# RWKV mixer in an encoder kernel: key order alternating by head pair, with whole-chunk handoffs

## What is computed

```
def step(S, inp):
    r_t, w_t, k_t, v_t, kk_t, b_t = inp
    sa = jnp.einsum('bhvk,bhk->bhv', S, -kk_t)
    S = S * w_t[:, :, None, :] + sa[..., None] * b_t[:, :, None, :] + v_t[..., None] * k_t[:, :, None, :]
    return S, jnp.einsum('bhvk,bhk->bhv', S, r_t)
...
y = head_norm(y, ln_g, ln_b, RW_GN_EPS)
y = y + jnp.sum(r * k * r_k.astype(F32), axis=-1, keepdims=True) * v
y = y.reshape(B, T, RW_WIDTH) * jax.nn.silu(g.astype(F32))
return y.astype(h.dtype) @ w_out
```

## Time and profile before

| | us |
|---|---|
| median of 3 runs | 1469.68 (1467.86 to 1470.78) |
| profiled execution | 1469.67 |
| its span | 1467.5 |
| TensorE busy | 1360.3 (93%) |
| VectorE busy | 717.9 (49%) |
| ScalarE busy | 400.5 (27%) |
| GpSimd busy | 90.6 (6%) |
| mean granted clock of TensorE | 0.975 |

### The profile page before, as it was taken

One profiled execution on the slowest core, in us unless ns is written; L12 is line 12 of the kernel. 1 busy time (PEld: TensorE's weight loads), 2 busy tenths in 40 slices (PEclk: granted clock), 3 DMA queues, 4 the chain that ended last, 5 costly groups with the idle time before them and its releaser, 6 DMA issues. The chain is left out here.

```text
span 1467.5 us, 23757 instructions
## 1 busy us (share of the span) xinstructions
PE 1360.3 (93%) x10291; PEld 715.9 (49%) x10291; DVE 717.9 (49%) x1388; ACT 400.5 (27%) x900; POOL 90.6 (6%) x82
## 2 busy tenths in 40 slices
PE   5999999999798999879899989998999999998887
PEld 3444444488444444564434436544444444477633
DVE  5784656855642002261345023434684765954552
ACT  1114243165301011460122053501113244055401
POOL 0000240100000000000000000000000152000000
PEclk9999999999899999999999989998999999999999
DMA  6222222001400222101222221123322222101211
GB/s 208 72 72 57 60 71 61 27 4 61 176 0 1 72 86 72 58 2 58 73 60 84 72 57 29 50 65 87 107 62 68 65 61 63 43 4 61 83 52 57
DMA packets 111183, 92.45 MB, mean 63 GB/s; under 512 B 5020, under 2 KB 99524, under 8 KB 110568
## 3 DMA queue, kind: packets, MB, share of 16 engines
q1 hardware_dynamic: 110376, 88.81, 19.9%
q10 hardware_dynamic: 704, 2.13, 0.4%
HBM read 84.64 MB, written 6.29 MB: 62 GB/s over the span
## 5 line engine op out<-in xcount | busy, mean ns | idle before, releaser
L871 PE MATMUL bank<-arena 128*128 128x512 f32 x960 | 420.1, 594 | 1.5 <-ACT arena L544 1.5
L871 PEld LDWEIGHTS bank<-arena 128*128 128x128 f32 x960 | 180.6, 190 | 224.9 <-issue 219.1
L826 PE MATMUL bank<-arena 64*64 64x64 f32 (+3 forms) x6720 | 187.3, 227 | 22.9 <-issue 16.2
L826 PEld LDWEIGHTS bank<-arena 64*64 64x64 f32 (+2 forms) x6720 | 164.2, 134 | 59.3 <-issue 48.3
L1200 PE MATMUL bank<-arena 128*128 128x512 f32 x256 | 116.3, 615 | 4.6 <-DVE arena L1165 4.6
L159 ACT ACTIVATE arena<-arena 128x1024 f32<-128x1024 f32 x20 | 21.1, 1055 | 243.1 <-DVE arena L1171 131.9
L1200 PEld LDWEIGHTS bank<-arena 128*128 128x128 f32 x256 | 50.0, 198 | 70.7 <-issue 64.3
L1664 PE MATMUL bank<-arena 128*128 128x512 f32 x160 | 71.2, 606 | 1.6 <-PEq L301 1.6
L637 DVE SCALAR_TENSOR_TENSOR arena<-arena 128x512 f32<-128x512 f32 x96 | 72.2, 803 | 0.0
L1296 PE MATMUL bank<-arena 128*128 128x512 f32 x128 | 56.8, 606 | 1.6 <-PEq L1109 1.6
L498 POOL MEMSET arena<- 128x8 f32 x2 | 0.2, 112 | 936.4 <-DVE arena L788 936.4
(11 more groups left out here) (232 smaller groups left out, 1615.3 us busy)
## 6 DMA issues: line engine op xcount, KB each, us to landing
arena<-in_rw_w_in SPq DMA_DIRECT2D x66, 512.0 KB, 4.0
arena<-in_ml_w_in SPq DMA_DIRECT2D x24, 512.0 KB, 3.8
arena<-in_sw_w_in SPq DMA_DIRECT2D x20, 512.0 KB, 3.7
arena<-in_rw_w_out SPq DMA_DIRECT2D x16, 512.0 KB, 7.4
spill<-arena SPq DMA_DIRECT2D x2, 2048.0 KB, 8.9
arena<-spill SPq DMA_DIRECT2D x2, 2048.0 KB, 8.6
arena<-in_sw_w_out SPq DMA_DIRECT2D x8, 512.0 KB, 3.7
arena<-in_ml_w_out SPq DMA_DIRECT2D x8, 512.0 KB, 3.7
```

What stands on the lines that cost most here:

```text
L826: mm = lambda out, a, b, start=True, stop=True: nc.tensor.matmul(out, a, b, start=start, stop=stop, skip_group_check=True)
L871: last = nc.tensor.matmul(bank[:, :], slot[:, k, :], mix_at[what][:, k, :], start=k == 0, stop=k == KT - 1)
```

## The change

The order of b and k in the 128 columns of a pair's keys alternates: even pairs hold b | k, odd pairs k | b. So one matmul with both keys as weights (64 rows, 128 columns) puts each result where the masks want it: two matmuls a pair instead of four, in `products_a` and `products_r`. `turn_values` makes both heads of a pair in one matmul. The right side's two parts and `solve` go by pairs of alternating parity, so that four pairs of row and column halves follow each other; they are handed over once a chunk, and the outputs from the state become a step of their own behind `solve`. `x(c + 1)` comes behind `turn_values(c + 1)`. The inverses are stored so that a chunk's block is contiguous. ACT: `keep_bkt` 2 copies instead of 6, `values` 2 instead of 4, `gather` 8 of half the size and 2 more instead of 4. POOL and DVE work on K and b in two halves by parity, and POOL's r_k product comes last. The reload of h moves to `rw_gate_out`, behind the loads of W; the add waits for it. The core of the diff, without context; the functions K(j), BB(j) and `of_parity` stand for the former slices elsewhere too:

```diff
-    KB = m.view(B_K, KT, NC, 2 * C)
-    K, BB = KB[:, :, :, C:P], KB[:, :, :, 0:C]
+    KB = m.view(B_K, KT // 2, NC * 2, P)
+    slots = m.view(B_K, KT // 2 * NC, 4, C)
+    both = lambda p, c: KB[:, p // 2, 2 * c + p % 2, :]
+    slot = lambda n: slots[:, :, n, :].rearrange("p (k c) d -> p k c d", c=NC)
+    tile_of = lambda at, j: slot(at(j % 2))[:, j // 2, :, :]
+    K_AT, B_AT = (lambda odd: 1 + odd), (lambda odd: 3 * odd)
+    K, BB = (lambda j: tile_of(K_AT, j)), (lambda j: tile_of(B_AT, j))
+    of_parity = lambda at, odd, c: slot(at(odd))[:, :, c, :]
+    parity = lambda buf, odd: buf.rearrange("p (k o) c -> p k o c", o=2)[:, :, odd, :]
+    in_parity = lambda buf, odd, c: parity(buf[:, :, span(c)], odd)
...
-            sp.wait_ge(rhs_done.handle, rhs_done.at(2 * BC))
+            sp.wait_ge(sa_done.handle, sa_done.at(NC))
+            m.load_weights(sp, n0 + 33 + SLOTS)
...
-            sp.dma_start(m.view(A_H, 4096), spill[0]).then_inc(reloaded.handle, 16)
...
-            sp.wait_ge(sa_done.handle, sa_done.at(2 * NC))
-            m.load_weights(sp, n0 + 33 + SLOTS)
-            sp.wait_ge(reloaded.handle, reloaded.at(16))
...
-                nc.gpsimd.tensor_tensor(R[:, :, span(c)], R[:, :, span(c)], K[:, :, c, :], ALU.mult).then_inc(rk_ready.handle, 1)
+                for odd in range(2):
+                    last = nc.gpsimd.tensor_tensor(in_parity(R, odd, c), in_parity(R, odd, c), of_parity(K_AT, odd, c), ALU.mult)
+                last.then_inc(rk_ready.handle, 1)
+                for odd in range(2):
+                    last = nc.gpsimd.tensor_tensor(of_parity(B_AT, odd, c), of_parity(B_AT, odd, c), parity(epi[c], odd), ALU.mult)
+                last.then_inc(b_scaled.handle, 1)
...
-                nc.gpsimd.tensor_tensor(BB[:, :, c, :], BB[:, :, c, :], epi[c], ALU.mult).then_inc(b_scaled.handle, 1)
...
-                    turned = blocks(t_bank(c, q))
-                    nc.scalar.activation(KB[:, pairs[q], c, 0:C], turned[:, :, 0:C], ACT.Copy)
-                    nc.scalar.activation(KB[HI, pairs[q], c, C:P], turned[LO, :, C:P], ACT.Copy)
-                    nc.scalar.activation(KB[LO, pairs[q], c, C:P], turned[HI, :, C:P], ACT.Copy).then_inc(bkt_evac.handle, 1)
+                    nc.scalar.activation(KB[:, 2 * q:2 * q + 2, 2 * c:2 * c + 2, :].rearrange("p a b c -> p a (b c)"),
+                                         t_bank(c, q)[:, :].rearrange("p (a b) -> p a b", a=2), ACT.Copy).then_inc(bkt_evac.handle, 1)
...
-                for g in range(4):
-                    rows, half = slice(Q * g, Q * g + Q), g % 2
-                    last = nc.scalar.activation(ad[rows, c // BC, :, KT * (c % BC):KT * (c % BC) + KT],
-                                                heads(ga[c], g // 2)[rows, :, Q * half:Q * half + Q]
-                                                .rearrange("p k c -> p c k"), ACT.Copy)
-                if c == NC - 1:
-                    last.then_inc(gathered.handle, 1)
+                at = KT * (c % BC)
+                for w in range(2):
+                    for half in range(2):
+                        for odd in range(2):
+                            mine, rows = slice(C * w + Q * half, C * w + Q * half + Q), slice(C * odd + Q * half, C * odd + Q * half + Q)
+                            nc.scalar.activation(ad[mine, c // BC, :, at + odd:at + KT:2],
+                                                 heads(ga[c], w ^ odd)[rows, odd:KT:2, Q * half:Q * half + Q]
+                                                 .rearrange("p k c -> p c k"), ACT.Copy).then_inc(gathered.handle, 1)
+                act.wait_ge(gathered.handle, gathered.at(8 * (c + 1)))
+                for odd in range(2):
+                    nc.scalar.activation(heads(ga[c], 1)[EARLIER[1 - odd], 1 - odd:KT:2, 0:Q],
+                                         heads(ga[c], 1)[EARLIER[odd], odd:KT:2, Q:C], ACT.Copy).then_inc(crossed.handle, 1)
...
-                for q in range(2):
-                    act.wait_ge(v_done.handle, v_done.at(2 * c + q + 1))
-                    nc.scalar.activation(heads(z[c], 0)[HI, pairs[q], :], quarter(m.bank[q])[HI], ACT.Copy)
-                    nc.scalar.activation(heads(z[c], 1)[LO, pairs[q], :], quarter(m.bank[q])[LO], ACT.Copy)\
-                        .then_inc(v_evac.handle, 1)
+                act.wait_ge(v_done.handle, v_done.at(c + 1))
+                for odd in range(2):
+                    rows = SIDE[1 - odd]
+                    last = nc.scalar.activation(both_heads(c, odd)[rows], wider(m.bank[0])[rows], ACT.Copy)
+                last.then_inc(v_evac.handle, 1)
...
-                for g in range(2):
-                    act.wait_ge(rhs_done.handle, rhs_done.at(2 * c + g + 1))
-                    nc.scalar.activation(rhs[:, pairs[g], :], quarter(m.bank[4 + g]), ACT.Copy, scale=-1.0)\
+                act.wait_ge(rhs_done.handle, rhs_done.at(c + 1))
+                for odd in range(2):
+                    nc.scalar.activation(parity(rhs, odd), quarter(m.bank[4 + odd]), ACT.Copy, scale=-1.0)\
...
-                for g in range(2):
-                    act.wait_ge(sa_done.handle, sa_done.at(2 * c + g + 1))
-                    for par, rows in SIDES:
-                        last = nc.scalar.activation(heads(z[c], par)[rows, pairs[g], :], quarter(m.bank[6 + g])[rows], ACT.Copy)
+                act.wait_ge(sa_done.handle, sa_done.at(c + 1))
+                for w in range(2):
+                    for odd in range(2):
+                        rows = SIDE[odd]
+                        last = nc.scalar.activation(head_of(c, odd, w ^ odd)[rows], quarter(m.bank[6 + w])[rows], ACT.Copy)
...
-                    nc.vector.transpose(tt[:, b], t32[:, b].rearrange("p t s -> p s t"))
-                    last = nc.vector.transpose(uu[:, b], t32[:, b])
+                    nc.vector.transpose(tt[:, b].rearrange("p n s -> p s n"), t32[:, b].rearrange("p t s -> p s t"))
+                    last = nc.vector.transpose(uu[:, b].rearrange("p n t -> p t n"), t32[:, b])
...
-                    rows, to, at = slice(Q * g, Q * g + Q), slice(Q * (g ^ 2), Q * (g ^ 2) + Q), Q * (g % 2)
-                    last = nc.vector.tensor_copy(u[c][to, :, at:at + Q], uu[rows, c // BC, :, KT * (c % BC):KT * (c % BC) + KT]
-                                                 .rearrange("p c n -> p n c"))
+                    rows, at = slice(Q * g, Q * g + Q), Q * (g % 2)
+                    last = nc.vector.tensor_copy(u[c][rows, :, at:at + Q], of_chunk(uu, c)[rows])
...
-                last = [None, None]
-                for slot, keys in ((0, BB), (1, K)):
-                    for par, rows in SIDES:
-                        out = (LO, HI)[par ^ slot]
-                        last[par] = mm(banks[par][out, C * p:C * p + C], keys[rows, p, c, :], query[rows, p, span(c)])
-                if p == KT - 1:
-                    for par in range(2):
-                        last[par].then_inc(inc.handle, 1)
+                for par, rows in SIDES:
+                    last = mm(banks[par][:, C * p:C * p + C], both(p, c)[rows], query[rows, p, span(c)])
+                    if p == KT - 1:
+                        last.then_inc(inc.handle, 1)
...
-                        last = nc.tensor.transpose(t_bank(c, q)[:, P * k:P * k + P], KB[:, 4 * q + k, c, :], ident)
+                        last = nc.tensor.transpose(t_bank(c, q)[:, P * k:P * k + P], both(4 * q + k, c), ident)
...
-                for q in range(2):
-                    for k in range(4):
-                        for par, rows in enumerate((HI, LO)):
-                            last = mm(m.bank[q][rows, C * k:C * k + C], V[:, 4 * q + k, span(c)], centre[:, C * par:C * par + C])
-                    last.then_inc(v_done.handle, 1)
+                for p in range(KT):
+                    last = mm(m.bank[0][SIDE[1 - p % 2], P * (p // 2):P * (p // 2) + P], V[:, p, span(c)], centre)
+                last.then_inc(v_done.handle, 1)
...
-            def x_begin(c):
+            def x(c):
...
-                    pe.wait_ge(ga_evac.handle, ga_evac.at(2 * NC))
+                    pe.wait_ge(crossed.handle, crossed.at(2 * NC))
...
+                for p in range(KT):
+                    for w in range(2):
+                        block = ga[c][EARLIER[w], 2 * p, Q:C] if w == p % 2 else ga[c][EARLIER[w], 2 * (p ^ 1) + 1, 0:Q]
+                        last = mm(x_bank[LATER[w], Q * p:Q * p + Q], block, of_chunk(tt, c)[EARLIER[w], p, :])
+                last.then_inc(x_done.handle, 1)
...
-            def x(c, p):
-                for par in range(2):
-                    last = mm(x_bank[LATER[par], Q * p:Q * p + Q], ga[c][EARLIER[par], 2 * p + par, Q:C],
-                              of_chunk(tt, c, p)[EARLIER[par]])
-                if p == KT - 1:
-                    last.then_inc(x_done.handle, 1)
...
-            def xu(c, p):
-                for par in range(2):
```

(69 more changed lines are left out.)

66 lines of the change are left out of this document (36 added, 30 removed).

## The result

The changed kernel takes 1462.31 us (median of 17 runs, 1460.65 to 1464.60), against 1469.68 for the kernel before (17 runs beside them). The ratio is 0.9948, 95% interval 0.9938 to 0.9957: faster by 0.5%, less than a third of the 24.7 us forecast and outside the range of 1436 to 1458.

A forecast was written before the change was run, and what follows sets the result against it. TensorE bounds the kernel, its chunk loop on the edge of its instruction fetch. Loop gain 25.2 us less 0.6 for the v stage makes 24.6, from 1469.68 to 1445 us; own range 1441 to 1449, whole range 1436 to 1458.

The forecast's parts named there:

- The products: Merged 64x128 instructions in `products_a` and `products_r`: 29 ns each, 0.93 us against 0.95 in the chunk loop, so nothing.
- part 1: The chunk loop of layers 1 and 4: periods fall to 9.9 us, gaining 11.8 and 13.4 us, 25.2 in all.
- part 2: The v projections alternating with `products_a`: -1.2 for POOL's earlier b, +1.5 for gather, +0.3 us a layer, range -1.5 to +3.
- Rival D: Merged products neither overlap nor hide their loads, 60 ns each: 1.92 against 0.95 us, 1474 us in all; chance 0.04.
- the ring: V stage cycle of mask, gather, exponentials, scale: its turn grows from 6.43 to 7.9 us, just under TensorE's 8.1.
- `x` and `xu`: In the chunk loop, as many instructions as before, right operand now contiguous; no gain taken.
- Rival A: `x` and `xu` speed up from 27 to 14.9 ns through contiguous reads, 0.8 us a period: 1439 us; chance 0.18.
- Right sides, `solve` and `state_outputs`: Chunk loop: each right side gains 0.45 us a period by four quadrants; `solve` then `state_outputs` lose 0.47.
- The fetch: Loading TensorE's own program, 3.6 us a block, stops the loop; 48 fewer pairs give 8.8 us a period, stops nearly vanish.
- Rival E: The fetch isn't what stops TensorE in the loop and the stops stay: 1458 us; chance 0.05.
- The period: One chunk of the loop, `turn_bk` to `turn_bk`: 10.26 us stall-free becomes 9.8, plus 0.1 of stops, 9.9.
- New waits of the loop, inversion, reload: `outputs` waiting for ACT copies: covered by 0.2 us; inversion, 1.5 later: hidden; h's reload in `rw_gate_out`: hidden, 20 us spare.

The follow-up runs named there:

- split_both: Changed kernel with each merged 64x128 product cut back into two 64x64 ones in both `products_a` and `products_r`: 1450.8 us, ratio 0.9867 to the kernel before.
- split_a: Changed kernel with 64x64 products in `products_a` alone, `products_r` still merged: 1453.7 us, ratio 0.9880 to the kernel before.
- split_a_spread: Changed kernel with `products_a` split into 64x64 and DVE's eight g mixes spread over chunks 1 to 3: 1441.59 us, ratio 0.9804 to the kernel before.
- strided_x: Changed kernel with the inverse's copy stored in the old layout, so `x` reads its moving operand with a stride: 1468.32 us, ratio 0.9985 to the kernel before.
- split_both_spread: Changed kernel with both products split as before the change and the g mixes spread over chunks 1 to 3: 1439.13 us, ratio 0.9781 to the kernel before.
- probe_shapes: Changed kernel with the instruction shapes of `products_a` varied by chunk, output wrong, only instruction times read: 27.4 to 101 ns an instruction.

## Why the prediction was wrong

By its steps, against 24.6 us of gain forecast and 5.9 in the span.

- **The products (part 1, and TensorE's side of part 2): the step that failed.** They were "Not in the trace in this size", with bounds of 29 and 60 ns an instruction, and the prediction took 29, by the 64*128 projections of the lora step, and so a cost of nothing. Measured: 57. Those projections move 512 columns, so that any load of weights vanishes behind the stream; they could say that row halves overlap, which they do, and nothing of the load. The row at the other end, 128 columns of weights with 4 moving in one tile, gave 60. Rival D, at a chance of 0.04, took this for every instruction, without overlap. It had the load right as the cause, but its price came near by luck: the row halves do overlap, and a load in one of them takes 112 ns, nearly twice what the earlier trace rows shows. The 60 with the overlap would have given 30, the forecast again, so no row quoted there had the price. D's cost of 0.97 a call was measured as 0.84; its sum of 1474 was too dark because in the loop the fetch would have taken nearly all of the 0.84 (a period of 10.38 in `split_both`, 10.21 to 10.4 in most of `split_a`), and not the 2 us for all calls that it allowed.
- **The v stage (part 2).** Forecast +0.3 a layer, measured +10.2 and +8.5 up to the loop. Of this, 6.7 is the products of the stage, and 0.84 more those of `products_r(0)`. The waits before came to 2.1 in this stretch and are 2.0 now, where the forecast let two of them "stay or grow by 0.5 to 1"; but the lower clock behind them, 2.4 + 0.9 us and 1.2 + 0.4, was in no term. `split_a_spread` shows that both are the block of g mixes. The term for the ring was right: gather of eight copies 3.5 us and crossing 0.64 (forecast 3.4 and 0.6), turn 8.0 for 7.9:

```profile
191.58 3.52 ACT L581 ACTIVATE arena<-arena 32x128 f32<-32x128 f32 x8 [9.62 <-DVE arena L675]
195.14 0.64 ACT L586 ACTIVATE arena<-arena 32x128 f32<-32x128 f32 x2
...
199.58 3.57 ACT L581 ACTIVATE arena<-arena 32x128 f32<-32x128 f32 x8 [2.15 <-DVE arena L675]
```

- **`x` and `xu` (part 1).** Forecast no gain, measured 32 ns for two instructions instead of 57: 0.39 and 0.37 a period. Rival A is true, at 0.18; `strided_x` shows the cause for `x`. This mended much of the first error in the loop.
- **Right sides, `solve` and `state_outputs`.** Both right sides and `solve` start four instructions every 58 ns, so four quadrants count as said, and `state_outputs` goes at 29 ns, as forecast. But the gain was 0.52 for both right sides and not 0.90. No term had the handoff within TensorE: `right_side_state` waits for the last product of `right_side_values` to be finished, now for all pairs at once, where the kernel before waited by groups and the first had long been done. The weight loads behind it stand 1.6 us in 301 to 384 us, once in each of seven periods (the row below); the kernel before has no such row. That is over half of what is missing, some 3.7 us of the kernel (an estimate, 16 x 0.23); leaving the wait by groups wasn't tried. `solve` with `state_outputs` lost 0.62 and not 0.47: between groups of different shape TensorE starts nothing for up to 0.15 us, and the sum had no term for that. By the Trainium skill's rule on row tiles and one bank (TensorEngine Tiling, Gotcha 1) the right side from the state should have stayed at 29 ns; it doesn't.

```profile
PEld bank L843 <- PE bank L843: 1.6, 7, 0.2
```

- **The fetch.** Right in mechanism and nearly in size. Stops fall from 6.1 to 0.3 us; they come back when 32 pairs are added (`split_both`); one block takes 3.8 to 3.9 us (`split_both`, `split_both_spread`) rather than 3.6. Rival E falls.
- **The period** was forecast at 9.9 and is 10.21: 6.6 us of the forecast gain are missing by this, and they lie in the steps named above.
- **New waits of the loop, inversion, reload.** No `outputs` waits for ACT in a full period; in the last chunk 0.87 and 0.74 us. The inversion stayed hidden, and so did the reload.
- **What wasn't in any term:** 5.0 us less between the layers. 1.5 is POOL's wait at the first product of the last layer, which the forecast had counted with the v stage; 1.7 is the layer of 182.5 against 184.2 us above, a matter of the clock. The other 1.8 are the clock as well: the first eight products of the gate stage take 3.67 us at a clock of 1.00 where they took 5.37 at 0.68, the last transposes ahead of layer 2 take 1.09 at 1.00 for 1.97 at 0.50, and against that the first products with W take 9.95 for 9.22. The change leaves these matmuls as they were, and why the clock falls in other places isn't known. So 3.5 of the 5.9 us of span came by luck, as far as this forecast goes.

## What to carry to other kernels

A matmul with few moving columns is priced by its weights: count columns loaded one after the other in each column tile, and don't merge two 64-column weights into one of 128 to save instructions; put the doubled operand on the moving side, if the users of the result can take it transposed. A row in which another quantity binds can't price a new shape, however alike it looks, and here the row with as many weight columns was wrong by two as well: where the bounds lie as far apart as 29 and 60 ns and the sum hangs on it, measure the shape first (`probe_shapes` has eight of them in one run). And before shortening an array-bound step, look at whether another limit (here the fetch of TensorE's program, some 3.8 us for 256 instructions) stands just beneath it: of two limits that close, lifting one gives only the distance to the other.

## What the hardware showed beyond that

- The load of weights on a 64-row tile takes 0.88 to 0.91 ns a column in f32 (112, 85 and 58 ns for 128, 96 and 64) and is hidden up to the length of the stream (128 columns of weights and 128 moving: 58 ns an instruction, as with 64 moving). The transposes of the earlier trace rows have 128 columns of weights and start every 60 ns; why they load nearly twice as fast is open.
- With a strided moving operand of 32 columns two instructions of `x` take 57 ns, with a contiguous one 32.
- Two row halves that write one bank, in different partitions (the right side from the state), start four instructions every 58 ns, as the products with two banks do.
- A wait of 2 to 3.6 us of TensorE at the third product was followed by the lower clock level and cost up to 3.3 us more; one of 1.3 us in the kernel before was not. But in `probe_shapes` one of 2.42 us was not either (clock 1.00, the v tile 7.13 us), and there the clock fell 20 us later, behind chunk 4, with no wait just before it (0.81 from 214.2 to 223 us). The length of one wait doesn't settle it.
